# A two-layer hybrid decoder step on one core: the first layer up to its attention is reordered over five engines

## What is computed

```python
a = rmsnorm(h, g_mix_pre[0])
z = a @ w_in_a[0]                       # 1024 -> 512 (u) + 3 x 512 (q, k, v)
u, qkv = z[..., :512], z[..., 512:].reshape(bsz, t, 3, 8, 64)
qm, km, vm = partial_rope(qkv[:, :, 0], pos), partial_rope(qkv[:, :, 1], pos), qkv[:, :, 2]
# s5_mixer: 32 groups x 16 channels, 64 complex states each
dt  = exp(log_dt); mag = exp(ar * dt)
abr, abi = mag * cos(ai * dt), mag * sin(ai * dt)      # the state's factor of one step
cr, ci = ((abr - 1) * ar + abi * ai) / den, (abi * ar - (abr - 1) * ai) / den
x = c * (u @ b)                                        # complex, 64 states of each group
h[t] = ab * h[t - 1] + x[t]                            # the recurrence
y = gelu(re(c_out * h) + d * u); y = y * sigmoid(y @ w_glu + b_glu)
```

## Time and profile before

| | us |
|---|---|
| median of 3 runs | 2087.26 |
| profiled execution's own time | 2080.89 |
| its span in the trace | 2079.1 |
| PE busy | 1912.2 (92% of the span) |
| DVE busy | 1131.7 (54%) |
| ACT busy | 717.4 (35%) |
| POOL busy | 13.7 (1%) |

### The profile page before, as it was taken

How to read it: one execution, slowest core, us unless ns; L and a number is a source line. 1 busy time by engine, 2 the same in 40 slices (tenths; PEclk the granted TensorE clock), 3 DMA queues, 4 the chain that set the end, 5 groups by cost and what they waited for, 6 DMA issues and landing times.

```text
span 2079.1 us, 34106 instructions
## 1 busy us (share of the span) xinstructions
PE 1912.2 (92%) x13244; PEld 1660.8 (80%) x13244; DVE 1131.7 (54%) x2433; ACT 717.4 (35%) x1300; POOL 13.7 (1%) x27
## 2 busy tenths in 40 slices
PE   6999889899999979999999898787799999979997
PEld 5587555798999979988489896344598999979987
DVE  7982154547777762253322395555557777762254
ACT  3211233454333342254322222444454333342252
POOL 0000000000000000000000000000000000000000
PEclk9999878899999999999999957799999999999998
DMA  4112457512222222131122310655212222222121
GB/s 165 62 43 86 159 175 275 198 42 71 92 81 81 68 102 81 55 114 62 44 88 82 110 48 10 238 205 201 82 48 72 87 86 81 68 97 83 56 81 46
DMA packets 77851, 204.12 MB, mean 98 GB/s; under 512 B 12530, under 2 KB 14754, under 8 KB 77218
## 3 DMA queue, kind: packets, MB, share of 16 engines
q1 hardware_dynamic: 75442, 189.70, 27.0%
q0 software_dynamic: 2288, 12.72, 1.7%
HBM read 190.81 MB, written 10.40 MB: 97 GB/s over the span
## 4 chain that ended last, share of the span: by engine, by line
PE 83%; DVE 12%; ACT 3%; issue 2%; DMA 1%; DVEq 0%; POOL 0%; ACTq 0%; POOLq 0%
PE psum L395 39%; PE psum L559 12%; PE psum L1491 6%; PE psum L403 5%; PE psum L2034 3%; PE psum L1235 2%; PE psum L790 2%; PE psum L1210 1%; PE psum L481 1%; PE psum L1328 1%; PE psum L1305 1%; PE psum L2175 1%; DVE sb_arena_r L355 1%; PE psum L495 1%; PE psum L1060 1%
## 5 line engine op out<-in xcount | busy, mean ns | idle before, releaser
L395 PE MATMUL psum<-sb_a_sb_r,sb_ring_r 128*128 128x288 f32 x1280 | 259.1, 295 | 0.0
L395 PE MATMUL psum<-sb_a_sb_r,sb_arena_r 128*128 128x288 f32 x1280 | 257.0, 296 | 0.0
L395 PE MATMUL psum<-sb_y_sb_r,sb_arena_r 128*128 128x288 f32 x704 | 207.1, 294 | 11.4 <-DVE sb_arena_r L355 11.2
L395 PE MATMUL psum<-sb_y_sb_r,sb_ring_r 128*128 128x288 f32 x704 | 208.6, 296 | 0.0
L395 PEld LDWEIGHTS psum<-sb_a_sb_r,sb_ring_r 128*128 128x128 f32 x1280 | 206.8, 188 | 0.0
L395 PEld LDWEIGHTS psum<-sb_a_sb_r,sb_arena_r 128*128 128x128 f32 x1280 | 204.2, 188 | 0.0
L355 DVE TENSOR_TENSOR sb_ring_r<-sb_ring,sb_ring_r 128x1024 fp32r<-128x1024 f32 (+1 forms) x78 | 101.6, 1306 | 159.6 <-ACT sb_ring_r L352 158.9
L352 ACT ACTIVATE sb_ring_r<-sb_ring 128x1024 fp32r<-128x1024 f32 (+1 forms) x78 | 87.4, 1124 | 286.3 <-PE psum L395 221.2
L559 PE MATMUL psum<-sb_arena_r 128*128 128x288 f32 x960 | 160.7, 302 | 8.3 <-DVE sb_arena_r L355 8.3
L395 PE MATMUL psum<-sb_arena_r,sb_ring_r 128*128 128x288 f32 x1056 | 145.4, 299 | 20.9 <-DVE sb_arena_r L355 20.9
L395 PEld LDWEIGHTS psum<-sb_arena_r,sb_ring_r 128*128 128x128 f32 x1056 | 143.6, 192 | 21.3 <-issue 21.3
(11 more groups left out here) (420 smaller groups left out, 3415.4 us busy)
## 6 DMA issues: line engine op xcount, KB each, us to landing
sb_ring<-w SPq DMA_DIRECT2D x166, 512.0 KB, 3.5
sb_ring<-wd SPq DMA_DIRECT2D x32, 704.0 KB, 4.1
sb_arena<-sb_v SPq DMA_DIRECT2D x64, 256.0 KB, 5.4
sb_arena<-moba_v SPq DMA_DIRECT2D x56, 256.0 KB, 5.0
sb_ring<-moba_k SPq DMA_DIRECT2D x32, 256.0 KB, 4.1
sb_a_sb<-moba_k SPq DMA_DIRECT2D x32, 256.0 KB, 5.4
sb_ring<-sb_k SPq DMA_DIRECT2D x32, 256.0 KB, 4.0
sb_a_sb<-sb_k SPq DMA_DIRECT2D x32, 256.0 KB, 5.4
```

What stands on the lines that cost most here:

```text
L395: ins = e.eng.matmul(out[:, half, :], fr(w[p][:, k, :]), fr(x[q][:, k, cols]), start=(first and k == 0 and i == 0), stop=(last and k == kb ...
```

## The change

What it does, part by part:

1. The sum over the 8 blocks of squares is made by seven DVE additions in place; PE does two matmuls in the place of 16.
2. The parameters move from DVE to POOL, whose program has no scalar_tensor_tensor, so that each of those becomes two operations (`mix`). The phases move to POOL too, and so does the memset of `mt`, behind them.
3. v's rows and q's and k's tiles become split products. v's weights are split by ACT within the u stage, after the first and the third of u's tiles; q's and k's by ACT (`act_split_rope`) two tiles ahead.
4. DVE's diagonal, states, scan, remainders of the q and k weights and rotation stand in one hand-made order (`dve_states_rope`); `hin` is written by the last addition and not by a copy. Complex products write their real part directly where they may (`apart=True`).
5. The 64-row matmuls of the kernel rows and of the output alternate between the lower and the upper 64 rows; in the output the 128-row matmuls of a tile come first.
6. SP holds the first weights back until the sixth block of x has landed, and issues three of the small loads; the last two weight slabs of q and k are loaded behind the 32 kernel transfers.

In the diff's core, `e.own is None` is true for POOL alone. `turn_back` first waits for `phases_ready`, with which the phases end; the phases first wait until the norm is done (`u_norm`):

```diff
+        def dve_norm_sum(e, sq):
+            for k in range(1, KD):
+                e.eng.wait_ge(sq_ready, k + 1)
+                ins = e.eng.tensor_tensor(sq[:, 0, :], sq[:, 0, :], sq[:, k, :], ALU.add)
+                if k < KD - 1:
+                    e.st.do(ins)
+                else:
+                    ins.then_inc(sq_sum, 1)
...
+        def mix(e, dst, x, c, z, first, second):
+            if e.own is None:
+                e.st.do(e.eng.tensor_scalar(u4, x, c, None, first))
+                e.st.do(e.eng.tensor_tensor(dst, u4, z, second))
+            else:
+                e.st.do(e.eng.scalar_tensor_tensor(dst, x, c, z, first, second))
...
         def dve_s5_tables(e):
+            v.wait_ge(params_ready, 1)
+            v.wait_ge(bc_in, 16 * 3)
...
         def pe_rope(e, acc):
-                    wait_slab(e, m)
+                    e.splits += 1
+                    e.eng.wait_ge(wl_ready, e.splits)
                     t = acc.next("act")
                     wait_emptied(e, t)
-                    mm_tile(e, pair(t.s), slabs[:, m], a, KD).then_inc(acc_ready, 1)
+                    mm_split(e, pair(t.s), split[m % 2], (y, a), KD).then_inc(acc_ready, 1)
...
         def pe_value_rows(e, acc):
                 for k in range(KD):
-                    last = e.eng.matmul(psum[0:n, 2 * t.s, :], x[:, k, i * P:i * P + n], slabs[:, slot:slot + 4, k, :],
-                                        start=(k == 0), stop=(k == KD - 1))
+                    for j, (x, w) in enumerate(((y, wh_rows), (y, slabs[:, 4:8]), (a, wh_rows))):
+                        last = e.eng.matmul(psum[0:n, 2 * t.s, :], fr(x[:, k, i * P:i * P + n]), fr(w[:, :, k, :]),
+                                            start=(k == 0 and j == 0), stop=(k == KD - 1 and j == 2))
...
         def dve_split_u(e, acc):
+            for j in range(4):
+                e.splits += 1
+                v.wait_ge(wh_ready, e.splits)
+                dve_low(e, slabs[:, 4 + j], wh_rows[:, j], slabs[:, 4 + j], wl_ready)
...
         def act_proj_u(e, acc):
                 if x[0] == "M":
+                    if j % 2 == 0:
+                        for i in (j, j + 1):
+                            wait_slab(e, 4 + i)
+                            act_high(e, slabs[:, 4 + i], wh_rows[:, i], wh_ready)
...
         def act_rope(e, acc):
                     wait_filled(e, t)
+                    if m + 2 < 8:
+                        act_split_rope(e, m + 2)
...
+        def dve_states_rope(e, acc):
+            low(0)
+            low(1)
+            diagonal(0)
+            diagonal(1)
+            own_states()
+            turn_back()
+            diagonal(2)
+            diagonal(3)
+            low(2)
+            scans()
+            low(3)
+            dve_rope(e, 0, turned[0])
+            turn_on(0)
...
         @block.gpsimd
-            for dst, name in S5_LOADS:
+            for dst, name in S5_LOADS[:3]:
                 eng.dma_start(dst, A[name]).then_inc(s5_in, 16)
+            e = Engine(eng, None, pool_step)
+            eng.wait_ge(con_in, 32)
+            dve_s5_params(e)
+            dve_s5_phases(e)
+            eng.wait_ge(acc_ready, 1 + 12 + 5 + 4)
+            eng.memset(mt_all, 0.0).then_inc(mt_zero, 1)
...
         @block.vector
-            dve_s5_params(e)
+            dve_norm_sum(e, a)
             dve_split_u(e, acc)
             dve_s5_tables(e)
             eng.drain().then_inc(tables_ready, 1)
-            dve_s5_phases(e)
-            dve_s5_states(e, acc)
-            dve_rope(e, acc)
+            dve_states_rope(e, acc)
```

More of the change, by code:

```diff
@@ L410, in pe_norm @@
             wait_emptied(e, t)
-            for k in range(KD):
-                e.eng.wait_ge(sq_ready, e.squares + k + 1)
-                for half in range(2):
-                    last = e.eng.matmul(pair(t.s)[:, half, :], ones, sq[:, k, half * HALF:(half + 1) * HALF],
-                                        start=(k == 0), stop=(k == KD - 1))
+            e.eng.wait_ge(sq_sum, 1)
+            for half in range(2):
+                last = e.eng.matmul(pair(t.s)[:, half, :], ones, sq[:, 0, half * HALF:(half + 1) * HALF], start=True, stop=True)
             last.then_inc(acc_ready, 1)
             e.squares += KD
+        def dve_norm_sum(e, sq):
[6 more added lines that the diff above has]
+                    ins.then_inc(sq_sum, 1)
         def act_norm(e, acc, src, sq, arrive):
@@ L601, in cmul @@
             e.st.do(tt(t[1], x[1], z[1], ALU.mult))
-            e.st.do(tt(t[0], t[0], t[1], ALU.add if conj else ALU.subtract))
+            e.st.do(tt(out[0] if apart else t[0], t[0], t[1], ALU.add if conj else ALU.subtract))
             e.st.do(tt(t[1], x[1], z[0], ALU.mult))
@@ L609, in cmul @@
                 e.st.do(tt(out[1], t[1], out[1], ALU.subtract if conj else ALU.add))
-            e.st.do(e.eng.tensor_copy(out[0], t[0]))
-        s5_in = sem("s5_in")
+            if not apart:
+                e.st.do(e.eng.tensor_copy(out[0], t[0]))
+        s5_in, bc_in, params_ready, phases_ready = sem("s5_in"), sem("bc_in"), sem("params_ready"), sem("phases_ready")
         (dt, adt, mag, mag8, kf, r, r2, sn, cs, nr, den, rden, crr, cii, u0, u1) = tiny[:16]
@@ L779, in pe_rope, with pe_value_rows @@
                     last.then_inc(acc_ready, 1)
-        def pe_value_rows(e, acc, slot, x):
-            for i in range(4):
-                wait_slab(e, slot + i)
+        def pe_value_rows(e, acc):
+            e.splits += 4
+            e.eng.wait_ge(wl_ready, e.splits)
             for i in range(5):
@@ L868, in act_rope, with rope_tiles @@
                     acc.next("dve")
[L870 to L874 removed]
+        def rope_tiles(acc):
+            turned = []
             for m in range(9):
@@ new lines, in scans, with turn_on @@
+            def scans():
+                do(v.tensor_copy(t0, mag8.unsqueeze(2).to_broadcast([P, GP, NC_P])))
+                do(v.memset(t0[:, :, 0:1], 0.0))
+                for z in gst:
+                    f = z.rearrange("p g c -> p (g c)")
+                    do(v.tensor_tensor_scan(out=f, data0=t0.rearrange("p g c -> p (g c)"), data1=f, initial=0.0,
+                                            op0=ALU.mult, op1=ALU.add))
+            def turn_on(i):
+                other, op = ((gi, ALU.subtract), (gr, ALU.add))[i]
+                do(tt(t0, gst[i], ph[0], ALU.mult))
+                do(tt(t1, other, ph[1], ALU.mult))
+                do(tt(hin[i][:, :, 1:NC_P], t0[:, :, 0:NC_P - 1], t1[:, :, 0:NC_P - 1], op))
+                do(tt(s5o[i][:, :, 0:1], t0[:, :, NC_P - 1:NC_P], t1[:, :, NC_P - 1:NC_P], op))
+                do(v.memset(hin[i][:, :, 0:1], 0.0))
+                do(v.tensor_copy(hin[i][:, :, NC_P:NCH], st0[i]))
@@ L1033, in sp_s5_kernels @@
+            low(6)
+            dve_rope(e, 3, turned[3])
+            low(7)
+            for m in range(4, 8):
+                dve_rope(e, m, turned[m])
         def sp_s5_kernels(ld):
```

225 lines of the change are left out of this document (126 added, 99 removed).

## The result

The changed kernel takes 2069.36 us (median of 8 runs, 2066.17 to 2072.45). The kernel before, on the same chip at the same time, takes 2083.80 (8 runs, 2078.79 to 2092.69). The ratio is 0.9928, 95% interval 0.9908 to 0.9947: 14.4 us faster, where I had forecast 34.8. The time lies inside my range of 2039 to 2082; the gain is about two fifths of the forecast. The time itself came nearer to the forecast (2069 against 2052) than the gain did, by luck: I started from the median of three runs, 2087.3, and with eight runs the kernel before takes 2083.8.

A forecast was written before the change was run, and what follows sets the result against it. PE was taken as the bound almost throughout from 37.5 to 243 us, behind POOL's loads and DVE. Terms -6.6 + 1.5 - 4.1 - 11.2 - 14.4 = -34.8 from 2087.3 gave 2052 us; 8-in-10 range 2039 to 2082.

The forecast's parts named there:

- POOL is hidden: GpSimd's parameters, phases and memset: phases done at 97, memset in time for PE, 7 us to spare.
- The norm: First layer's norm on VectorE: starts at about 18.4 instead of 23.70, of which 5.0 us were taken as gained.
- v's rows: Value rows on PE: 120 matmuls of 220 ns, 26.4 us for 34.53, PE done at 86.5.
- Tables: VectorE's tables before the states' stage: start at 49.6, last 40.2, end at 89.8, or 93 with sharing.
- the 3 us that I had allowed for sharing: Added to the tables' end for POOL working on the same memory, moving it from 89.8 to 93.
- S: Start of the states' stage on PE, after the tables: moves from 99.6 to 93.0, 6.6 us gained.
- States' stage: PE from S: 16.1 us of states before the q product; 1.5 us given back to low clock after PE's wait.
- The kernel rows: 64 matmuls in the states' stage, row halves side by side: 7.0 us for 11.12, 4.1 gained.
- q and k: Eight product tiles on PE from 7.76 to 6.36 us each, 11.2 gained; VectorE stays 2 to 5 us ahead.
- The output: Output stage on PE: a tile of eight from 7.6 to 4.0 us, four tiles 14.4 gained.
- The gate: Stage with the output, before attention: its 18.19 us stay, nothing gained.
- exclusion: Rival: POOL does one operation per VectorE table operation, PE waits 13.7 before the first rotation; gain 17, 2070 us; chance 0.22.

The follow-up runs named there:

- e1: The changed kernel with the memset of the kernel block moved back from GpSimd to VectorE; 2061.67 us, ratio 0.9882.
- u1: e3 with the eight q,k products in single precision in one pass again; 2058.86 us.
- e2: e1 with VectorE's order changed: third and fourth diagonal and third remainder ahead of the turning back, later remainders each a place earlier; 2056.22 us, ratio 0.9876.
- e3: e2 with the angles of the state-space parameters moved from GpSimd back to VectorE; 2050.70 us, ratio 0.9851, and once more 2052.95, ratio 0.9854.
- a2: The changed kernel, unaltered, run once more for a second profile; 2072.77 us (6 runs).
- r1: The kernel before with only the row order changed, in the kernel rows and the output stage; 2064.83 us, ratio 0.9904.
- p1: The changed kernel with extra memsets, copies and additions on GpSimd beside VectorE's table operations, as a probe; the one run took 2069.5 us.
- r2: r1 run once more, unaltered, for a second profile; 2064.72 us (5 runs).

## Why the prediction was wrong

The sum was 34.8 up to attention. Measured there: 20.0. The step that failed is *POOL is hidden*: GpSimd's chain was not done before PE needed it, and with the memset behind it, it held PE for 12.4 us. Step by step, in the profiled execution:

- *The norm*: at 17.11; I had 18.4. That is 1.3 better, from two misses. The last square ends at 12.06 and not 14.10: x is there earlier, which I had at nothing (that SP's held-back weights do it is likely, but no run takes them alone). PE's sum ends 3.4 us behind it, at 15.51, and not 2.5 as before.
- *v's rows*: tiles 5.57 apart, 232 ns a matmul; I had 220. PE done at 86.6; I had 86.5. That agreement is luck: PE began at 58.5 instead of 60.1, and the rows took 1.7 longer.
- *Tables*: the first miss. I had GpSimd's parameters done at 38 and the tables started by ScalarE at 49.6. VectorE was ready at 48.4, but the parameters were done only at 53.7. They began at 7.25 and not 5.5. Their step was about 0.3 with VectorE idle (I had 0.35), but mostly 0.6 to 0.9 beside VectorE's additions of the squares (up to 13 us) and 0.7 to 1.2 beside its norm and remainders (17 to 35 us). The tables, started at 54.15, then took 40.8 to PE's start, without the 3 us that I had allowed for sharing. S 94.95 instead of 93.0: 1.9 us. The start was 4.6 late; the allowance, not needed, hid the rest.
- *States' stage*: 18.5 from S to the first q product, where I had 16.1: the transposes at low clock cost 2.4, for which my sum had 1.5: 0.9 us. The kernel rows' 7.0 was right (7.1).
- *POOL is hidden with 7 us to spare*: this is the step that failed. I saw that the two share memory, and priced it as a lump of 15 us on the phases and nothing on the parameters, without asking how many GpSimd operations fit beside VectorE's. It was one per long VectorE operation. The phases ended at 120.6 and not 97: 15.7 of these 23.6 us are the parameters, which released them at 53.7 and not 38, and 7.9 the phases themselves, 66.9 instead of 59 with the lump. The memset was done at 124.3, where 107.3 was the latest harmless time, and PE waited 12.4 before the first rotation, plus 2.8 for a rotation and a product at low clock behind it (2.29 and 7.81 for 0.97 and 6.38). e1 shows that the memset's place behind this chain made the whole of this wait; with the memset away, the late phases still cost 3.3.
- *q and k*: 6.38 a tile without gaps, as forecast; u1 confirms 1.38 a tile. That VectorE stays 2 to 5 us ahead of PE was not right by itself: the 12.4 us gave it time here, and without them PE waited 2.2 to 3.3 us for it (e1, e2, e3).
- *The output*: 3.8 a tile, forecast 4.0. (A tile is eight groups; the 0.95 is what one group takes, one 128-row matmul and two 64-row ones, and not a pair of groups as I wrote. The sum had eight.) *The gate*: 2.4 that I had not counted, the clock's in this execution (0.7 in a2's).

The misses are 1.9 + 0.9 + 12.4 + 2.8 - 0.8 (output) - 2.4 (gate) = 14.8, which is what was missing. With the memset and the angles moved and VectorE's order changed, e3 comes to a median of 2051.6 over its 8 runs, 33 us under before. That it is my 2052 is in part coincidence: its attention is 37 to 40 us earlier than before, more than my 34.8, as its tables start at 48.2 and not 49.6, and some of it is lost again behind. Nevertheless the q and k products and the order of row halves were each worth what I had said (u1, r1), and GpSimd's chain kept the whole from it.

The rival *exclusion* had the mechanism: it gave PE's wait as 13.7 (12.4 measured) and 2070 (2069.4 measured, though by 20.0 us at attention, where it had 17, and a loss behind it that it did not have). I gave it 0.22, because most GpSimd operations are short; but an operation's length doesn't matter when each has to wait for the end of another engine's. Its count was near too: 53 phase operations by the tables' end, 47 measured. One half of it was wrong where it mattered: I let a GpSimd operation hold VectorE by 0.15 each, 4 us in all, and VectorE lost nothing in the wide table operations; it lost 1.5 us later, beside GpSimd's wide ones. The section of the Trainium skill that I cited (SBUF - State Buffer, Who interferes with whom) says that of a two-input VectorE operation and a reading GpSimd one, the second waits. The trace agrees: beside VectorE's long operations the waiting one is GpSimd each time, and beside GpSimd's operations of 512 columns it is VectorE (113.59 above). GpSimd's memsets did not wait (p1). The price that the skill has for GpSimd (GPSIMD Engine Reference, Performance versus the Vector engine), twice VectorE's time for an addition, fits the wide additions: 1.28 and 1.30 for 512 columns against VectorE's 0.69 (products 1.05 to 1.10); for 16 columns the chained step is 0.29 to 0.34 against 0.21, that is 1.4 to 1.6 times.

The last 5 us, between 20.0 at attention and 14.4 in the medians, no part of my sum could have held: I took everything behind attention as unchanged, in time as well as in work. Their cause stays open.

## What to carry to other kernels

Before work goes to GpSimd beside VectorE, count GpSimd's operations that read, not their time: beside long two-input VectorE operations it gets one done for each of them. Ask the reverse too, where VectorE's operations are the short ones. Move writes there, or work that falls where VectorE idles, and never put the release of another queue (here a memset that SP waits for) behind such a chain. Price each part alone: here one of six parts, the order of row halves, carried the whole gain, and the others together paid only after the memset, VectorE's order and the angles had been moved (e1 to e3).

## What was not expected of the hardware

- GpSimd operations that read wait out each of VectorE's long two-input operations (2.21 to 2.56 instead of 0.21), a copy as well as an addition. GpSimd's memsets don't (0.16 for 16 columns, 0.56 for 512), and VectorE's memset of 4096 columns (3.47) doesn't hold GpSimd (0.40 to 0.46 for 128 columns beside it). The other way round, two VectorE additions of 128 columns took 2.15 instead of 0.62 beside GpSimd's products of 512 columns.
- The same program's time behind one mark varies by 8.5 us from execution to execution (r1 and r2, at mean granted clocks of 0.942 and 0.935), and the mark itself by up to 4.1 (e3). A difference of 5 us between two versions can be that alone in a single profile.
